# GLA and mLSTM values in a hybrid decoder layer: feature tiles transposed on TensorE in place of token tiles with meta passes

## The chip, the cores and the metric

One core of a Trainium2 chip runs the whole layer. The metric is the device time of one execution in microseconds (us); the time before is the median of three runs.

## What is computed

The input is 512 tokens of width 1024, with 16 learned meta tokens put ahead of them, so 528 rows go through the layer. One projection `z = rms_norm(h) @ w_in + b_in` feeds three mixers (GLA, sparse attention, mLSTM) and three gates. Cut to what matters:

```python
z = xn @ p["w_in"] + p["b_in"]          # 528 x 9696, split into the parts below
# GLA: 4 heads, dk = 128, dv = 256
o = q exp(G) S + (q decay k) v          # S collects k exp(..) v over the chunks
# mLSTM: 4 heads, dk = 128, dv = 256; q, k through a causal convolution and silu
h = (w_inter q C + P v) / max(|den|, exp(-m))   # P = decay * (q k^T)
mix = sig(gate_a) (gla @ w_br_gla) + sig(gate_b) (dsa @ w_br_dsa) + sig(gate_c) (ml @ w_br_ml)
h = h + rms_norm(mix @ w_out); h = h + rms_norm(relu(rms_norm(h) @ w_up)^2 @ w_down)
```

The values `v` of GLA and of mLSTM are 1024 columns of `w_in` each, 256 a head. Everything is float32, to float32 accuracy.

## The kernel before

**Precision.** Every large product is made of three matmuls in the faster float32 format: weight high part by activation high part, high by low, low by high (`whi`, `wlo`, `xh`, `xl`). Smaller products and all transposes are plain float32.

**Weights.** SP loads chunks of 512 KB into three raw buffers (`wraw`). GpSimd splits each one (L619 the high part, L623 the low part in four pieces) into one of four pairs of buffers, in the order of `plan()` (L135 to L286). It may start when the last tile that used the buffers has signalled `gemm_done` (L616 to L618). The DMA of a raw buffer waits for `split_done` (L535).

**Tiles.** A tile is a product into one of two PSUM slots `GP`, in turn (L144 to L149). It waits until its slot is empty (`gfree`, L1857) and its chunk split (L1859), and signals `gemm_done` (L1897). Kinds:
- F, features by tokens: the stationary operand is a weight block of 128 columns, the moving one the activations, 512 columns (L1873), or with `both` twice 264 columns, so that the meta tokens are among them (L1870). 8 blocks of the contraction by 3 parts.
- V, tokens by features: the stationary operand is 128 tokens, the moving one 256 weight columns (L1888). Tile A has the first two blocks of tokens, tile B the other two: 48 matmuls each.
- VM and VT (tile M): the 16 meta tokens of GLA, or the last 16 tokens for mLSTM, whose blocks begin at the first meta token. Their high and low parts lie side by side in `xm` (32 columns), so it takes 16 matmuls (L1879, L1880).
- G: the forget gate of GLA from rank 16 (L1894).

`all_values` (L224) makes A, B and M of a head from one pair of chunks. VectorE moves A and B to `vh` with the bias `vb` added (L1392) and M to `vm` (L1397).

**The order of the work** is written out by hand for each engine. `nxt(kind)` on TensorE runs the next head's tile of this kind, or in the last head a tile of the gates (`ta`, `tc`), so that projections fill the time in which other engines work for this head.
- GLA (L2204 to L2251), for each head: q and k of the next head, seven levels of decayed scores with projections between them, A of the next head around level 6, transposes of the decayed keys (L2235, L2237), B around the states (L2242 to L2247), M, then `weighted`, the output products (L2181).
- mLSTM (L2294 to L2326), for each head: q of the next head, scores 0 and 1, k of the next head, scores 2 and 3, A of the next head, the recalled products of scores and values (L2291, L2292), the sums over weights (L2322, L2324), then B and M of the next head.

ScalarE and VectorE have orders of their own. What the prediction's steps touch: on ScalarE the GLA loop (L929 to L961) with `off_out` (L879, keys out of PSUM), and the mLSTM loop (L1057 to L1087) with `conv_in` (L988), `conv_sig` (L996, sigmoid), `out_gate` (L1039), `lnexp` (L638, which loads the table for exp and ln) and `head_squares` (L1049). On VectorE `off` (L1489, its end are the states, L1502, L1508), the mLSTM loop (L1731 to L1756) with `weights_of` (L1688), `weight_sums` (L1696 to L1700), `conv` (L1658, L1660), `low_parts` (L1540) and `conv_mul` (L1671, L1673).

The part of the mLSTM loop of ScalarE that matters most:

```python
            if more:
                conv_sig(h + 1, 1)
            lnexp()
            if not more:
                gate_in("tc", 16, 2)
            head_squares(h)
```

Of the kernel before, what the change touches and what calls it, by code (L numbers as in the profile page):

```python
# [69 lines left out]
def _rows():  # L70
    at = 0
    for name, n, src in [
        ("gq", 4, "b_in"), ("gk", 4, "b_in"), ("gr", 8, "b_in"), ("cq", 2, "b_in"), ("ckv", 1, "b_in"),
        ("ik", 1, "b_in"), ("mq", 4, "b_in"), ("mk", 4, "b_in"), ("mo", 8, "b_in"), ("gate", 24, "b_in"),
        ("a2", 4, "b_gla_a"), ("hg", 2, "g_gla_head"),
        ("hm", 2, "g_ml_head"), ("dq", 2, "g_dsa_q"), ("dkv", 1, "g_dsa_kv"), ("ig", 1, "idx_ln_g"),
        ("ib", 1, "idx_ln_b"), ("fb", 1, "ml_f_bias"), ("cv", 32, "ml_conv"),
    ]:
        ROWS[name] = at
        ROW_LIST.append((name, n, src))  # L80
        at += n
    return at
# [6 lines left out]
JOINED = {"gq": 8, "cq": 3, "mq": 8}  # L89
FOLLOWS = ("gk", "ckv", "mk")  # L90
# [21 lines left out]
NROWDMA = 22  # L112
# [22 lines left out]
def plan():  # L135
# [27 lines left out]
    def values(name, c0):  # L163
        c = [chunk("w_in", c0, P), chunk("w_in", c0 + P, P)]
        assert c[0] % 2 == 0
        tile(name + "A", c, 0, kind="V", off=0)
        tile(name + "B", c, 0, kind="V", off=2)
        tile(name + "M", c, 2, kind="VT" if name[0] == "m" else "VM")

    def pad():  # L170
        if len(chunks) % 2:
            chunks.append(None)

# [50 lines left out]
    def all_values(name, c0):  # L224
        pad()
        values(name, c0)

    gla(0)
    all_values("gv0", C_GV)
    for h in range(HEADS):  # L230
        if h + 1 < HEADS:
            gla(h + 1)
        else:
            gates("ta", C_GATE, 0, 2)
        pairs("gr", C_GR, h)
        if h + 1 < HEADS:
            all_values(f"gv{h + 1}", C_GV + (h + 1) * DV)
# [6 lines left out]
    all_values("mv0", C_MV)  # L244
    for h in range(HEADS):
        if h + 1 < HEADS:
            feature(f"mq{h + 1}", "w_in", C_MQ + (h + 1) * DK, both=True)
            feature(f"mk{h + 1}", "w_in", C_MK + (h + 1) * DK, both=True)
        else:
            gates("tc", C_GATE + 2 * D, 0, 2)  # L250
        if h + 1 < HEADS:
            all_values(f"mv{h + 1}", C_MV + (h + 1) * DV)
# [37 lines left out]
def build(nc, a, line, scratch, rows, out):  # L290
# [3 lines left out]
    with ctx:  # L294
# [6 lines left out]
        def region(offset, specs):  # L301
# [23 lines left out]
        xm = sb("xm", [P, KT, 2 * META], F32R)  # L325
# [44 lines left out]
        (sgate, gtmp, vb, qh, ATm, kh, vh, vm, AT, sqo, rso, on, km) = region(AO, [  # L370
            ("sgate", [P, 2, SEQ], FP32), ("gtmp", [P, 2, SEQ], FP32), ("vb", [P, D], FP32),
# [3 lines left out]
        BO = AO + (2 * SEQ * 2 + D + 2 * SEQ + 2 * ALL + 2 * QT * DV + 2 * DV + QT * SEQ + SEQ + 2 * SEQ + SEQ + 2 * SEQ + 2 * P) * 4  # L375
# [16 lines left out]
        (sqr,) = region(AO + (7 * SEQ + D + 2 * ALL + 2 * QT * DV + 2 * DV + QT * SEQ) * 4, [("sqr", [P, 2, SEQ], F32R)])  # L392
        (qg,) = region(AO + (4 * SEQ + D) * 4, [("qg", [P, 2, QT, P + P // 2], FP32)])
# [17 lines left out]
        def gate_store(m):  # L411

            return [vh[:, 0, 0:2, :].rearrange("p a b -> p (a b)"), vh[:, 0, 2:4, :].rearrange("p a b -> p (a b)"),
                    kh[:, 0, 0:SEQ], qh[:, 0, :], vb[:, 0:SEQ], vb[:, SEQ:D], AT[:, 0, :], AT[:, 1, :]][m]
# [61 lines left out]
        ld_v, zpad, cv_ok, cs_ok, qk_ok = sem("ld_v"), sem("zpad"), sem("cv_ok"), sem("cs_ok"), sem("qk_ok")  # L476
# [3 lines left out]
        xt_ok, ml_c = sem("xt_ok"), sem("ml_consts")  # L480
# [147 lines left out]
        def _(act):  # L628
# [41 lines left out]
            def input_high(t):  # L670

                if t == QT:
# [3 lines left out]
                    act.wait_ge(xh_ok, KT + 1)  # L676
                    nc.scalar.activation(xm[:, :, 0:META], xh[:, :, 0:META].bitcast(FP32), ACT.Copy).then_inc(xh_ok, 1)
# [167 lines left out]
            act.dma_start(vb[:, :], a["b_in"][0:1, C_GV:C_GV + D].broadcast_to([P, D])).then_inc(ld_a, 16)  # L845
# [81 lines left out]

            gate_of(0)
            for h in range(HEADS):  # L929
                last = h == HEADS - 1  # L930
                level(h, 0)
                if h:
                    squared(h - 1)
                level(h, 1)
# [20 lines left out]
                off_out(h)  # L955
                sigmoids(h)
                if last:

                    whole("gv3M")
# [20 lines left out]
            act.dma_start(vb[:, :], a["b_in"][0:1, C_MV:C_MV + D].broadcast_to([P, D])).then_inc(ld_v, 16)  # L980
# [64 lines left out]
            fetch_maxima(0)  # L1045
            def head_squares(h):
# [10 lines left out]
            for h in range(HEADS):  # L1057
# [27 lines left out]
                if not more:  # L1085
                    gate_in("tc", 16, 2)
                head_squares(h)  # L1087
            gate_in("tc", 16, 3)
            whole("mv3M")
# [88 lines left out]
        def _(dve):  # L1178
# [45 lines left out]
            def input_low(t):  # L1224
                if t == QT:
# [3 lines left out]
                    dve.wait_ge(xl_ok, KT + 1)  # L1229
                    nc.vector.tensor_copy(xm[:, :, META:2 * META], xl[:, :, 0:META].bitcast(FP32)).then_inc(xl_ok, 1)  # L1230
# [155 lines left out]
            dve.wait_ge(ld_a, 48)  # L1386

            def values(name, h, part):
                if part < 2:
                    t = tl[f"{name}{h}{'AB'[part]}"]  # L1390
                    ps = ready(f"{name}{h}{'AB'[part]}")
                    tt(vh[:, h % 2, 2 * part:2 * part + 2, :], ps[:, 0:2 * DV].rearrange("p (t n) -> p t n", t=2),  # L1392
                       vb[:, h * DV:(h + 1) * DV].unsqueeze(1).broadcast_to([P, 2, DV]), ALU.add).then_inc(gfree[t.slot], 1)
                    return
                ps = ready(f"{name}{h}M")
                dve.wait_ge(f16_ok, 2)
                stt(vm[0:2 * META, h % 2, :], vb[0:2 * META, h * DV:(h + 1) * DV], first16[:, :], ps[0:2 * META, 0:DV], ALU.mult, ALU.add).then_inc(gfree[tl[f"{name}{h}M"].slot], 1)  # L1397
# [91 lines left out]
            def off(h):  # L1489
# [6 lines left out]
                if h + 1 < HEADS:  # L1496
                    values("gv", h + 1, 0)
# [55 lines left out]
            for part in range(3):  # L1553
                values("gv", 0, part)
            for h in range(HEADS):
# [33 lines left out]
                if more:  # L1589
                    values("gv", h + 1, 1)  # L1590
                    values("gv", h + 1, 2)
# [5 lines left out]
            def gate_rows_of(m):  # L1597
# [18 lines left out]
                if m == 3:  # L1616
                    dve.wait_ge(gemm_done, tl["gv3M"].val)
                    nc.vector.tensor_copy(xm[:, :, 0:META], xh[:, :, SEQ:ALL].bitcast(FP32)).then_inc(xt_ok, 1)
                    nc.vector.tensor_copy(xm[:, :, META:2 * META], xl[:, :, SEQ:ALL].bitcast(FP32)).then_inc(xt_ok, 1)
# [4 lines left out]
                if m == 5:  # L1624
                    nc.vector.tensor_copy(later[:, 0:DIAG[0]], later_bigT[:, META:P])
# [102 lines left out]
            dve.wait_ge(ld_v, 16)  # L1728
            for part in range(3):
                values("mv", 0, part)  # L1730
# [110 lines left out]
        def _(pe):  # L1841
# [9 lines left out]
            def gemm(name, part=None):  # L1851
# [22 lines left out]
                elif t.kind in ("V", "VM", "VT"):  # L1874
                    s0 = chunks[t.chunks[0]]["hl"]
                    if t.kind != "V":
                        for k in range(KT):
                            w = slice(k * P, (k + 1) * P)
# [574 lines left out]
```

## Time and profile before

| | us |
|---|---|
| median of 3 runs | 1264.04 (1263.27 to 1264.69) |
| the profiled execution | 1264.5 |
| its span, first to last instruction | 1261.8 |

Busy time in the span:

| engine | us | share |
|---|---|---|
| TensorE matmul | 1253.5 | 99% |
| TensorE weight load (beside matmuls) | 1029.2 | 82% |
| GpSimd | 772.8 | 61% |
| VectorE | 629.2 | 50% |
| ScalarE | 392.9 | 31% |

PE is TensorE's matmul, PEld its weight load, DVE VectorE, ACT ScalarE, POOL GpSimd; L1888 is line 1888 of the kernel before. Matmuls overlap: a printed duration runs from the start of one to its modelled end, and the next one starts earlier, so the time that a matmul takes of the engine is the distance between starts. Plain float32 matmuls are two records each, transposes one.

### The profile page before, as it was taken

How to read it: one execution, taken by the hardware profiler on the slowest of the kernel's cores; microseconds unless marked ns; L12 is line 12 of the kernel's file. 1: busy time of each engine (PE TensorE's matmuls, PEld its weight loads, DVE VectorE, ACT ScalarE, POOL GpSimd, SP SyncE). 2: the span in 40 equal slices, each digit the busy share in tenths (PEclk: the TensorE clock that was granted, in tenths of full speed). 3: DMA queues.
4: the chain of work that ended last, by engine and by line, in shares of the span. 5: the costliest groups of instructions: out<-in, count | busy, mean ns of one | idle time of the engine just before them, and what ended most of it. 6: DMA issues, size and time to landing. Idle time of an engine off the chain costs nothing.

```text
span 1261.8 us, 17439 instructions
## 1 busy us (share of the span) xinstructions
PE 1253.5 (99%) x6561; PEld 1029.2 (82%) x6564; DVE 629.2 (50%) x1115; ACT 392.9 (31%) x810; POOL 772.8 (61%) x914
## 2 busy tenths in 40 slices
PE   9999999999999999999999999999999999999998
PEld 8866887677899899888899987887888888888886
DVE  4368888642276886835447773342511112333434
ACT  5343565533023323333024343312511111221322
POOL 8746430125584753758775556784876677888882
PEclk9999999999999999999999999999999999999999
DMA  7847200223231322322433333522233333232321
GB/s 177 241 122 224 68 1 26 68 67 94 71 97 51 84 62 56 84 68 84 117 110 78 86 97 100 188 95 84 84 101 100 85 100 105 96 100 84 101 84 67
DMA packets 167433, 120.08 MB, mean 95 GB/s; under 512 B 11367, under 2 KB 145613, under 8 KB 167350
## 3 DMA queue, kind: packets, MB, share of 16 engines
q1 hardware_dynamic: 160612, 107.79, 29.7%
q10 hardware_dynamic: 6738, 11.18, 2.7%
q8 instruction: 52, 0.85, 0.3%
q14 instruction: 31, 0.25, 0.1%
HBM read 114.71 MB, written 9.62 MB: 99 GB/s over the span
## 4 chain that ended last, share of the span: by engine, by line
PE 99%; DVE 0%; ACT 0%; issue 0%; DVEq 0%; ACTq 0%
PE GP L1873 46%; PE GP L1909 9%; PE PA L1909 9%; PE GP L1888 7%; PE GP L1870 6%; PE PA L2073 3%; PE GP L2135 3%; PE PA L2173 1%; PE PA L2110 1%; PE PA L2291 1%; PE GP L2366 1%; PE GP L1954 1%; PE PA L2043 1%; PE PA L2283 1%; PE PA L2074 1%; PE GP L1880 1%
## 5 line engine op out<-in xcount | busy, mean ns | idle before, releaser
L623 POOL TENSOR_TENSOR wlo<-wraw,whi 128x256 fp32r<-128x256 f32 x708 | 564.7, 828 | 14.7
L619 POOL TENSOR_SCALAR whi<-wraw 128x1024 fp32r<-128x1024 f32 x177 | 201.1, 1136 | 449.9 <-PE GP L1873 227.2
L1873 PE MATMUL GP<-xh,whi 128*128 128x512 f32 x352 | 144.8, 411 | 0.0
L1873 PE MATMUL GP<-xh,wlo 128*128 128x512 f32 x352 | 139.1, 395 | 0.0
L1873 PE MATMUL GP<-xl,whi 128*128 128x512 f32 x352 | 138.8, 394 | 0.0
L1815 DVE TENSOR_TENSOR ul<-U,uh 128x512 fp32r<-128x512 f32 x64 | 65.2, 1054 | 109.5 <-ACT uh L1157 109.5
L1873 PE MATMUL GP<-nh,whi 128*128 128x512 f32 x240 | 95.1, 396 | 0.0
L1873 PE MATMUL GP<-nl,whi 128*128 128x512 f32 x240 | 95.1, 396 | 0.0
L1873 PE MATMUL GP<-nh,wlo 128*128 128x512 f32 x240 | 95.1, 396 | 0.0
L1819 DVE SCALAR_TENSOR_TENSOR U<-GP,rrow 128x512 f32<-128x512 f32 x32 | 22.1, 692 | 141.7 <-PE GP L1873 140.3
L1873 PEld LDWEIGHTS GP<-xh,whi 128*128 128x128 f32 x352 | 66.2, 188 | 16.0 <-issue 1.5
L1873 PEld LDWEIGHTS GP<-xh,wlo 128*128 128x128 f32 x352 | 66.1, 188 | 15.2
L1873 PEld LDWEIGHTS GP<-xl,whi 128*128 128x128 f32 x352 | 66.3, 188 | 14.3 <-issue 0.5
L1157 ACT ACTIVATE uh<-U 128x512 fp32r<-128x512 f32 x64 | 37.2, 625 | 129.0 <-PE PA L1909 70.4
L1873 PE MATMUL GP<-yh,whi 128*128 128x512 f32 x192 | 76.3, 397 | 0.0
L1873 PE MATMUL GP<-yl,whi 128*128 128x512 f32 x192 | 76.1, 396 | 0.0
L1873 PE MATMUL GP<-yh,wlo 128*128 128x512 f32 x192 | 76.1, 396 | 0.0
L1888 PE MATMUL GP<-whi,xh 128*128 128x256 f32 x256 | 74.6, 292 | 0.2 <-DVE kh L1403 0.2
L1888 PE MATMUL GP<-wlo,xh 128*128 128x256 f32 x256 | 71.9, 281 | 0.0
L1888 PE MATMUL GP<-whi,xl 128*128 128x256 f32 x256 | 71.7, 280 | 0.0
L1161 ACT ACTIVATE U<-U 128x512 f32<-128x512 f32 x32 | 20.2, 632 | 152.9 <-DVE U L1819 152.9
L1873 PEld LDWEIGHTS GP<-nh,wlo 128*128 128x128 f32 x240 | 45.2, 188 | 11.0
(426 smaller groups left out, 2771.5 us busy)
## 6 DMA issues: line engine op xcount, KB each, us to landing
wraw<-in_w_in SPq DMA_DIRECT2D x75, 512.0 KB, 3.9
wraw<-in_w_up SPq DMA_DIRECT2D x32, 512.0 KB, 4.0
wraw<-in_w_down SPq DMA_DIRECT2D x32, 512.0 KB, 3.5
line_rows<-bias_line SPq DMA_DIRECT2D x8, 655.0 KB, 5.1
table<-line_rows SPq DMA_DIRECT2D x4, 1024.0 KB, 5.6
wraw<-in_w_br_dsa SPq DMA_DIRECT2D x8, 512.0 KB, 4.2
wraw<-in_w_br_gla SPq DMA_DIRECT2D x8, 512.0 KB, 3.9
wraw<-in_w_br_ml SPq DMA_DIRECT2D x8, 512.0 KB, 4.0
```

The costliest lines, as they stand in the source:

```text
L619: nc.gpsimd.tensor_scalar(hi, src, 1.0, 1.0, ALU.mult, ALU.mult).then_inc(hi_done, 1)
L623: part = nc.gpsimd.tensor_tensor(lo[:, at:to], src[:, at:to], hi[:, at:to].bitcast(FP32), ALU.subtract)
L1157: nc.scalar.activation(uh[:, k % 4, :], U[:, k % FT, :], ACT.Copy).then_inc(uh_ok, 1)
L1161: nc.scalar.activation(U[:, m, :], U[:, m, :], ACT.Square).then_inc(U_ok, 1)
L1815: tt(ul[:, k % 4, :], U[:, k % FT, :], uh[:, k % 4, :].bitcast(FP32), ALU.subtract).then_inc(ul_ok, 1)
L1819: stt(U[:, m, :], ps[:, 0:SEQ], 0.0, rrow[:, :], ALU.max, ALU.mult).then_inc(gfree[tl[f"up{m}"].slot], 1)
L1870: ins = mm(ps[0:t.m, b * SEQ:b * SEQ + HALF], wt[:, s0, w], hx[:, k, b * HALF:(b + 1) * HALF], start=st, stop=sp_)
L1873: ins = mm(ps[0:t.m, 0:SEQ], wt[:, s0, w], av, start=st, stop=sp_)
L1888: ins = mm(o_, at_[:, k, tok], wt[:, s0:s0 + 2, k * P:(k + 1) * P], start=(k == 0 and p_ == 0), stop=(k == KT - 1 and p_ == 2))
L1909: ins = mm(accumulators(name, hf, i), av[:, i * P:(i + 1) * P], wt[:, c["hl"], k * SEQ:(k + 1) * SEQ], start=(n == 0 and k == 0 and p_ == ...
L2073: mm(bank(v % 2)[0:r, 0:w], qlat[:, h, TILE_AT[i]:TILE_AT[i + 1]], kvT[:, 0:w], start=True, stop=False)
L2135: ins = mm(pairs_of(o_, g), kvn[:, j, :], pairs_of(PT[:, g % 2, j, :], g), start=(j == 0), stop=(j == i))
```

## The change

The values become F tiles with `both`, two of 128 features for a head (`gv00`, `gv01`, ...), with the meta tokens among their 528 columns. ScalarE copies each to a new buffer `vT` and adds the bias there (`value_in`). A new kind of tile T transposes `vT` on TensorE in four blocks of 128 tokens and one of 16 columns (the meta tokens for GLA, the last tokens for mLSTM), five transposes into a slot of `GP`; it waits for the copy of its F tile (`evacuated`). The T tiles are copied to `vh` and `vm` by VectorE, in GLA the second half by ScalarE (`values_copied`). Tiles V, VM and VT, `xm`, `vb`, its two broadcast DMAs and the pairing of chunks go; the biases of values and of two more row groups come with rows that are loaded anyway, so SP issues 20 row DMAs in place of 22. Cut to its core:

```diff
+    def turned(name, v):
+        tile(f"{name}T{v}", [], 0, kind="T")
...
+    def value(name, c0, h, v):
+        feature(f"{name}{h}{v}", "w_in", c0 + (2 * h + v) * P, both=True)
...
     def input_high(t):
...
-                    act.wait_ge(xh_ok, KT + 1)
-                    nc.scalar.activation(xm[:, :, 0:META], xh[:, :, 0:META].bitcast(FP32), ACT.Copy).then_inc(xh_ok, 1)
...
-            act.dma_start(vb[:, :], a["b_in"][0:1, C_GV:C_GV + D].broadcast_to([P, D])).then_inc(ld_a, 16)
...
+            def value_in(name, h, v):
+
+                if h:
+                    act.wait_ge(gemm_done, tl[f"{name}{h - 1}T{v}"].val)
+                t = tl[f"{name}{h}{v}"]
+                nc.scalar.activation(two(vT[:, v, :]), halves(ready(f"{name}{h}{v}")), ACT.Identity,
+                                     bias=cc(name, 2 * h + v)).then_inc(gfree[t.slot], 1)
+
+            def values_copied(h):
+
+                ps = ready(f"gv{h}T1")
+                nc.scalar.activation(vh[:, h % 2, :, P:DV], ps[:, 0:SEQ].rearrange("p (t n) -> p t n", t=QT), ACT.Copy)
+                nc.scalar.activation(vm[0:META, h % 2, P:DV], ps[0:META, SEQ:SEQ + P], ACT.Copy).then_inc(gfree[tl[f"gv{h}T1"].slot], 1)
...
             gate_of(0)
+            value_in("gv", 0, 0)
+            value_in("gv", 0, 1)
             for h in range(HEADS):
                 last = h == HEADS - 1
                 level(h, 0)
                 if h:
                     squared(h - 1)
+                values_copied(h)
                 level(h, 1)
...
                 off_out(h)
+                if not last:
+                    value_in("gv", h + 1, 0)
                 sigmoids(h)
+                if not last:
+                    value_in("gv", h + 1, 1)
...
+            value_in("mv", 0, 0)
+            value_in("mv", 0, 1)
...
                 if more:
                     conv_sig(h + 1, 1)
                 lnexp()
-                if not more:
+                if more:
+                    value_in("mv", h + 1, 0)
+                else:
                     gate_in("tc", 16, 2)
                 head_squares(h)
+                if more:
+                    value_in("mv", h + 1, 1)
...
+            def values(name, h, v):
+
+                ps, c = ready(f"{name}{h}T{v}"), slice(v * P, (v + 1) * P)
+                nc.vector.tensor_copy(vh[:, h % 2, :, c], ps[:, 0:SEQ].rearrange("p (t n) -> p t n", t=QT))
+                nc.vector.tensor_copy(vm[0:META, h % 2, c], ps[0:META, SEQ:SEQ + P]).then_inc(gfree[tl[f"{name}{h}T{v}"].slot], 1)
...
                 masked(h)
                 if h:
                     head_scaled(h - 1)
+                values("mv", h, 1)
                 for j in range(2):
                     weights_of(h, j)
...
                     conv(h + 1, 1)
-                    values("mv", h + 1, 0)
                     conv_mul(h + 1, 1)
                 denominator(h)
                 head_sums(h)
                 if more:
-                    for part in range(1, 3):
-                        values("mv", h + 1, part)
+                    values("mv", h + 1, 0)
...
+                elif t.kind == "T":
+                    v, first = int(name[4]), 0 if name[0] == "m" else META
+                    few = slice(SEQ, ALL) if name[0] == "m" else slice(0, META)
+                    evacuated(name[0:3] + name[4])
+                    for i in range(QT):
+                        nc.tensor.transpose(ps[:, i * P:(i + 1) * P], vT[:, v, first + i * P:first + (i + 1) * P], ident[:, :])
+                    ins = nc.tensor.transpose(ps[0:META, SEQ:SEQ + P], vT[:, v, few], ident[:, :])
...
-                nxt("gvA", 0)
+                nxt("gv0", 0)
                 level(h, 6)
-                nxt("gvA", 1)
+                nxt("gv0", 1)
...
-                nxt("gvB", 0)
+                nxt("gv1", 0)
...
-                nxt("gvB", 1)
-                nxt("gvM")
+                nxt("gv1", 1)
+                nxt("gvT0")
                 pe.wait_ge(od_q, 6 * h + 6)
                 weighted(h).then_inc(av_ps, 1)
+                if h + 1 < HEADS:
+                    gemm(f"gv{h + 1}T1")
...
                 nxt("mq", 1)
+                gemm(f"mv{h}T1")
...
-                nxt("mvA")
+                nxt("mv0")
                 pe.wait_ge(at_ok, 5 * h + 5)
...
-                nxt("mvB")
-                nxt("mvM")
+                nxt("mvT0")
+                nxt("mv1")
```

## Rows read from the trace of the kernel before

**Rows 1.** The page: busy time of the engines, and TensorE's granted clock in 40 slices.
```profile
PE 1253.5 (99%) x6561; PEld 1029.2 (82%) x6564; DVE 629.2 (50%) x1115; ACT 392.9 (31%) x810; POOL 772.8 (61%) x914
...
PEclk9999999999999999999999999999999999999999
```

**Rows 2.** Waits of TensorE, longest first: us in total, times, longest us.
```profile
PE PA L1930 <- DVE ones L1202: 1.2, 1, 1.2
```

**Rows 3.** Timeline of TensorE, mLSTM's third loop: start us, us, engine, line, operation, operands, count.
```profile
718.11 0.41 PE L1870 MATMUL GP<-xl,whi 128*128 128x264 f32 x2
...
720.78 1.69 PE L2283 MATMUL PA<-qh,kh 128*128 128x512 f32 x4
...
729.19 0.28 PE L1888 MATMUL GP<-wlo,xh 128*128 128x256 f32 x1
...
734.72 2.39 PE L2291 MATMUL PA<-AT,vh 128*128 128x512 f32 x8
...
740.22 0.59 PE L1888 MATMUL GP<-whi,xh 128*128 128x256 f32 x1
...
746.19 0.28 PE L1879 MATMUL GP<-whi,xm 128*32 128x256 f32 x1
...
748.04 0.40 PE L1873 MATMUL GP<-xh,whi 128*128 128x512 f32 x1
```

**Rows 4.** Timeline of TensorE in GLA: transposes of the keys, and the matmul behind.
```profile
445.25 0.30 PE L2235 MATMUL PA<-ident,km 128*128 128x128 f32 x1
...
445.39 0.49 PE L2237 MATMUL PA<-ident,KHt 128*128 128x128 f32 x3
...
445.64 0.36 PE L1888 MATMUL GP<-whi,xh 128*128 128x256 f32 x1
```

**Rows 5.** Timelines of TensorE and ScalarE, mLSTM's first and second loop.
```profile
673.12 0.59 PE L1888 MATMUL GP<-whi,xh 128*128 128x256 f32 x1
...
674.95 1.03 ACT L1049 ACTIVATE sqo<-PA 128x1024 f32<-128x1024 f32 x1
...
706.67 0.59 PE L1888 MATMUL GP<-whi,xh 128*128 128x256 f32 x1
...
708.91 1.03 ACT L1049 ACTIVATE sqo<-PA 128x1024 f32<-128x1024 f32 x1
```

**Rows 6.** Timelines of VectorE and ScalarE, mLSTM's third loop.
```profile
735.53 1.29 DVE L1540 TENSOR_TENSOR yl<-on,yh 128x512 fp32r<-128x512 f32 x2
...
738.09 2.38 DVE L1660 SCALAR_TENSOR_TENSOR cv<-zc,col,cv 128x528 f32<-128x528 f32 x3
...
736.20 0.68 ACT L988 ACTIVATE zc<-GP,col 128x528 f32<-128x528 f32 x1
...
740.50 0.65 ACT L996 ACTIVATE sgc<-cv 128x528 f32<-128x528 f32 x1 [2.58 <-DVE cv L1660]
...
741.17 1.28 ACT L638 ACT_TABLE_LOAD   x1
...
742.46 1.03 ACT L1049 ACTIVATE sqo<-PA 128x1024 f32<-128x1024 f32 x1
```

**Rows 7.** Timelines of VectorE and GpSimd, beside a split, and GpSimd's wait.
```profile
543.37 2.69 DVE L1540 TENSOR_TENSOR yl<-on,yh 128x512 fp32r<-128x512 f32 x2
...
630.56 3.45 DVE L1660 SCALAR_TENSOR_TENSOR cv<-zc,col,cv 128x528 f32<-128x528 f32 x3
...
630.32 4.29 POOL L623 TENSOR_TENSOR wlo<-wraw,whi 128x256 fp32r<-128x256 f32 x4
...
748.37 1.87 POOL L619 TENSOR_SCALAR whi<-wraw 128x1024 fp32r<-128x1024 f32 x1 [14.92 <-PE GP L1880]
```

**Rows 8.** Timelines of ScalarE, VectorE and TensorE, GLA's second loop.
```profile
445.92 0.60 ACT L879 ACTIVATE AT<-PA 128x512 f32<-128x512 f32 x1 [5.86 <-PE PA L2237]
...
450.08 1.58 DVE L1508 SCALAR_TENSOR_TENSOR AT<-AT,gf,PA 128x256 f32<-128x256 f32 x3
...
453.13 0.28 PE L1879 MATMUL GP<-whi,xm 128*32 128x256 f32 x1
```

More of the change, by code:

```diff
@@ L222, in gates @@
             feature(f"{name}{m}", "w_in", c0 + m * P)
-    def all_values(name, c0):
-        pad()
-        values(name, c0)
+    def value(name, c0, h, v):
+        feature(f"{name}{h}{v}", "w_in", c0 + (2 * h + v) * P, both=True)
     gla(0)
-    all_values("gv0", C_GV)
+    value("gv", C_GV, 0, 0)
+    value("gv", C_GV, 0, 1)
+    turned("gv0", 0)
+    turned("gv0", 1)
     for h in range(HEADS):
@@ L243, in plan @@
     feature("mk0", "w_in", C_MK, both=True)
-    all_values("mv0", C_MV)
+    value("mv", C_MV, 0, 0)
+    value("mv", C_MV, 0, 1)
+    turned("mv0", 0)
     for h in range(HEADS):
-        if h + 1 < HEADS:
+        more = h + 1 < HEADS
+        if more:
             feature(f"mq{h + 1}", "w_in", C_MQ + (h + 1) * DK, both=True)
+        else:
+            gates("tc", C_GATE + 2 * D, 0, 1)
+        turned(f"mv{h}", 1)
+        if more:
             feature(f"mk{h + 1}", "w_in", C_MK + (h + 1) * DK, both=True)
-        else:
-            gates("tc", C_GATE + 2 * D, 0, 2)
-        if h + 1 < HEADS:
-            all_values(f"mv{h + 1}", C_MV + (h + 1) * DV)
+            value("mv", C_MV, h + 1, 0)
+            turned(f"mv{h + 1}", 0)
+            value("mv", C_MV, h + 1, 1)
+        else:
+            gates("tc", C_GATE + 2 * D, 1, 2)
     gates("tc", C_GATE + 2 * D, 2, 8)
@@ L1084, in _ @@
                 lnexp()
-                if not more:
+                if more:
+                    value_in("mv", h + 1, 0)
+                else:
                     gate_in("tc", 16, 2)
                 head_squares(h)
+                if more:
+                    value_in("mv", h + 1, 1)
             gate_in("tc", 16, 3)
-            whole("mv3M")
             gate_in("tc", 16, 4)
@@ L1552, in _ @@
             forget_sums(0)
-            for part in range(3):
-                values("gv", 0, part)
+            values("gv", 0, 0)
             for h in range(HEADS):
@@ L1727, in _ @@
             dve.wait_ge(ml_c, 2)
-            dve.wait_ge(ld_v, 16)
-            for part in range(3):
-                values("mv", 0, part)
+            values("mv", 0, 0)
             for h in range(HEADS):
@@ L2268, in _ @@
             gemm("mk0")
-            for nm in ("mv0A", "mv0B"):
+            for nm in ("mv00", "mv01", "mv0T0"):
                 gemm(nm)
-            pe.wait_ge(xt_ok, 2)
-            gemm("mv0M")
             pe.wait_ge(M_ok, 1)
@@ L2298, in nxt @@
                     else:
-                        gemm({"mq": "tc0", "mk": "tc1", "mvA": "tc2", "mvB": "tc3", "mvM": "tc4"}[kind], part)
+                        gemm({"mq": "tc0", "mk": "tc1", "mv0": "tc2", "mvT0": "tc3", "mv1": "tc4"}[kind], part)
                 pe.wait_ge(qk_ok, 2 * h + 2)
```

95 lines of the change are left out of this document (26 added, 69 removed).

## Prediction

> **What bounds the kernel now.** The page comes first. TensorE is busy 1253.5 of the 1261.8 us span, the next engine 772.8 us, and the granted clock is at its full level (2.4 GHz) in all 40 slices [rows 1]. The list of waits, asked for TensorE alone, then shows that its longest wait is 1.2 us, at the start [rows 2]. So no wait sets this time, only TensorE's own stream: what leaves the stream comes off, and every new wait in it is paid in full, since nothing behind it has slack to give back. I therefore count pitches (start to start) in TensorE's timeline, not the printed durations, which overlap. Then I ask of each new wait in the stream when its releaser is ready.
>
> **1. Meta passes out.** A head's pass is 16 matmuls, from 746.19 to the next tile at 748.04 [rows 3]: 1.85 us. Eight heads: -14.8 us.
>
> **2. Values in feature layout.** A head has 96 matmuls either way: two 128-wide tiles of 8 x 3 x 2 halves, against four token tiles of 8 x 3. They stream 264 columns instead of 256. Pitch before: 47 matmuls between 729.19 and 734.72, 0.118 us. A tile that is already in the new form: 22 matmuls between 718.11 and 720.78, 0.121 us [rows 3]. Over 768 matmuls at 3.7 ns: +2.8 us.
>
> **3. Transposes in.** There are two tiles of five per head, 16 tiles. The nearest rows are the four transposes of the decayed keys, 445.25 to 445.64, so 0.39 us, the last three in 0.25 [rows 4]. A fifth adds 0.08; the matmul behind them shows 0.36 instead of 0.28, a change-over. I take 0.50 us a tile, +8.0 us. Below: five at 0.083, 0.41 us (+6.6). Above: 0.39 + 0.08 + 0.08 + as much again ahead of them, and a bit for two waits, 0.70 us (+11.2).
> The printed duration of one of these transposes is 0.30 us [rows 4], and at 0.27 to 0.30 each, if they did not overlap, 80 of them would be some 22 us. The Trainium skill (TensorE: Matmul & The Clock Gate, Part 4) speaks against this change there: about 275 ns for a transpose in a kernel's context. By it the sum would be 14 us higher. The trace has three inside 0.25 us, so I go by the pitch and keep the rule as a rival.
>
> Parts 1 to 3: -4.0 us of stream.
>
> **4. The new wait, mLSTM.** For heads 1 to 3 the tile mvT0 stands right behind the recalled products and the sums over weights, where the second half of the token tiles stood: at 673.12, 706.67 and 740.22 [rows 5, 3]. It may start only when ScalarE has copied the feature tile into vT. In ScalarE's queue that copy stands behind the sigmoid of the second convolution and the table load. That sigmoid starts at 740.50 and the load at 741.17; the next instruction, before which the new copy is put, starts at 742.46 [rows 6]. The copy has the shape of the conv input copy, 128x528 out of PSUM, 0.68 us [rows 6]; with its hand-over I take 0.70. vT is ready at 743.16. TensorE is there at 740.22 + 0.16 (48 columns x 8 longer, part 2) = 740.38. It waits 2.8 us. In the other heads the instruction behind the load starts at 674.95 and 708.91 [rows 5]: 675.65 - 673.28 = 2.4 and 709.61 - 706.83 = 2.8. Together +7.9 us. None of it is covered: the next tile (mv1) stands behind the transposes in TensorE's queue, and needs the slot that the same copy frees. The fourth head has gates there and doesn't wait. The chain to that sigmoid (scores, weights, their sums, two convolutions on VectorE) is not edited, so it does not come sooner.
>
> **5. What stretches that chain.** GpSimd splits the next weights when a chunk's last tile is done. Before, the pair of a head's values was held until the meta pass had run; GpSimd then waited 14.92 us for it [rows 7]. Now the first value tile's chunk comes free when that tile ends, at about 734.72 + 0.16 [rows 3], in the midst of VectorE's chain. Beside a split VectorE is slower: three convolution steps took 3.45 us while GpSimd split (630.3 to 634.6) and 2.38 us without [rows 7, 6]; the two subtractions to yl took 2.69 us beside a split and 1.29 us in this chain [rows 7, 6]. Both in full: +1.4 and +1.1 us in the second and third loop, +1.1 in the first, which has no subtractions; with the small steps up to 6.5 us in all. Below it is 0. A split is 4.3 us of subtractions behind a rounding of up to 1.87 [rows 7], so it ends about where the chain did; the last steps of a chain that has been stretched run alone. I take two thirds, +4.5 us.
>
> **6. GLA and the starts.** There the copy of the first half is put behind the key copy, 445.92 to 446.52 [rows 8], so vT is ready at 447.3, ahead of T0 at about 453.3, where the meta pass stood (453.13 and 0.17 for the longer columns) [rows 8]. The second half's copy ends 0.7 us behind its tile, and T1 stands behind the 32 output products, which are longer than that. VectorE's states end at 451.66 [rows 8] and are needed behind T0, at 453.8; that 2.1 us has to take in a split that now begins with the end of the first value tile, ahead of 445.25 [rows 4]. ScalarE's extra copies, two of 0.68 [rows 6], one of 0.60 [rows 8] and a small one a head, stand where it waits for VectorE; VectorE loses a pass over 128x512 a head. I cost all this at nothing; if the 2.1 us did not do, it would be up to 1 us a head. The two starts have no such work between: T1 of head 0 waits for a copy that can start only when its tile ends (0.7 against a T0 of 0.5), the next tile waits for VectorE to empty T0, and in mLSTM mq1 waits for the slot of mv01 in the same way. Each 0.2 to 0.3: +0.8 us, between 0 and 1.5. Queues: SP issues two row DMAs fewer, ScalarE's two broadcasts of the value biases go, and with them VectorE's copies to xm; no TensorE wait stood on any of them, so nothing.
>
> **Sum:** -4.0 + 7.9 + 4.5 + 0.8 = +9.2 us. The profiled execution took 1264.5 us (span 1261.8), 0.5 above the median of 1264.04; on the median this is **1273.2 us**, slower.
>
> **Rivals.**
> - *No stretch*: the wait is as worked out, but the split costs the chain nothing. +4.7, 1268.7 us. For it: the rows with a split have it beside the whole step, here it may run out early.
> - *The wait isn't there*, the side of faster: ScalarE's copy is done when TensorE arrives. Its place is the one of part 4; it decides at a chain 2.8 us shorter. Then -4.0 + 0.8 = -3.2, 1260.8 us. For it: VectorE drops an addition of 128x512 from this part of its queue. Against it: that addition stands behind the sigmoid's releaser, so its loss shortens nothing ahead.
> - *The clock falls* in the three waits of 4 us or so. TensorE has no wait over 1.2 us now and the clock stays at full level [rows 1, 2], so no row gives the price. Bounds: 0, and the value tile behind each wait (5.8 us) at half speed, 17.4 us. Half of it: 1282 us. The Trainium skill has such a rule (same page, "Why this matters for your kernels"): long idle gaps of TensorE between bursts of matmuls bring back the half clock, so they are to be avoided. By it this case would be likelier the more part 5 adds to the waits; no row here shows it.
> - *Transposes at their printed duration*: +13.8, 1287 us. Against it: three in 0.25 us [rows 4].
> - That the change doesn't do what it says: the stream without the meta passes is in the diff, 128 matmuls of 6561 [rows 1]; I see no way that they stay.
>
> **How the numbers follow.** A measurement of this kernel tells apart about 0.2%, 2.5 us. Forecast 0.55, no stretch 0.2, clock 0.08, no wait 0.07, transposes 0.03; the last 0.07 for sums that happen to land near zero, waits half hidden. Even the low ends (transposes at 0.41, no stretch) leave -5.4 + 7.9 + 0.8 = +3.3, above 2.5, so the first two cases count as slower. Slower 0.86, same 0.06, faster 0.08. Range: the low end is no stretch with the cheapest transposes, 1267.3; the high end takes full stretch and transposes at 0.70 (+5.2) and the mild part of the clock's case: 1267 to 1280.
>
> **What would show it.** Right: TensorE's list of waits has three entries at the transposes' line, released by ScalarE's value copy, of 2.4 us and up, and none above 0.5 in GLA; the meta pass's lines are gone; five transposes take 0.5 us; the convolution steps beside a split take over 1 us each. Wrong: no wait at that line, or the clock below full level behind it, or a wait in GLA at the output products.

## The result, and the profile after

| | before | after |
|---|---|---|
| median of the runs, us | 1263.76 (1263.27 to 1264.69, 4 runs) | 1280.83 (1279.81 to 1283.10, 4 runs) |
| span of the profiled execution, us | 1261.8 | 1279.0 |
| mean granted clock of TensorE | 1.000 | 0.993 |

The changed kernel takes 1.0135 times as long (95% interval 1.0122 to 1.0148): 17.1 us slower, where 9.2 were forecast and 1280 was the top of the range. The direction and the place were right, the size was not.

The page after the change, the answer to [rows 1]: TensorE's busy time, the slices of the granted clock, and the chain that ended last.

```profile
PE 1256.7 (98%) x6513; PEld 1031.2 (81%) x6516; DVE 617.5 (48%) x1112; ACT 405.4 (32%) x833; POOL 774.2 (61%) x914
...
PEclk9999999999999999999999889999999999999999
...
PE 95%; DVE 3%; ACT 1%; issue 1%; DVEq 0%; ACTq 0%
```

Two things are new. Two slices show the clock below full, both in mLSTM (a slice is 32 us; the two run from 703 to 767 us, and the one before them, with 0.95, still prints as a 9). And the chain that ended last runs through VectorE for 3% of the span, where TensorE alone had set the end.

The first of TensorE's list of waits, ahead of the one of [rows 2] (waiting line, releaser, us in total, times, longest):

```profile
PE GP L1885 <- ACT vT L933: 13.5, 4, 4.9
```

The wait that part 4 named is there: the transposes' line, released by ScalarE's copy into vT. TensorE's timeline at the three places, the answer to [rows 3, 5] (rounds one, two and three below are the first three passes of the mLSTM loop; start, us, engine, line, operation, operands, count, and in brackets the idle time with its releaser). L2322 is the last of the sums over weights, L1885 the transposes of T0, L2192 the squares in the middle of the next query's projection; the last row is the first gate tile behind mv31.

```profile
672.08 0.85 PE L2322 MATMUL PA<-Wd,ones 128*128 128x400 f32 x2
676.25 0.63 PE L1885 MATMUL GP<-ident,vT 128*128 128x128 f32 x4 [3.32 <-ACT vT L933]
...
687.12 0.40 PE L2192 MATMUL PA<-sqr,onesr 128*128 128x512 f32 x1
...
710.30 0.85 PE L2322 MATMUL PA<-Wd,ones 128*128 128x400 f32 x2
716.07 1.09 PE L1885 MATMUL GP<-ident,vT 128*128 128x128 f32 x4 [4.92 <-ACT vT L933]
...
727.75 0.40 PE L2192 MATMUL PA<-sqr,onesr 128*128 128x512 f32 x1
...
750.96 0.85 PE L2322 MATMUL PA<-Wd,ones 128*128 128x400 f32 x2
756.73 1.08 PE L1885 MATMUL GP<-ident,vT 128*128 128x128 f32 x4 [4.92 <-ACT vT L933]
...
765.63 0.40 PE L1879 MATMUL GP<-xh,whi 128*128 128x512 f32 x1
```

Before, the row that follows the sums started 0.38 us behind them (739.84 to 740.22). Now it is 4.17, 5.77 and 5.77 us. The difference is what TensorE loses: 3.8 + 5.4 + 5.4 = **14.6 us**. (The brackets say 0.47 less each, since they count from the modelled end of the matmul before.) The four transposes took 1.08 us in the third round, and in GLA, behind no wait, 0.60; so something else is slower too. Two windows of 11 us, around and behind the transposes of the second and the third round: width, busy times of PE, PEld, DVE, ACT and POOL, granted clock, DMA share, GB/s.

```profile
715.00:726.00 11.00, 9.93 (x63) 9.88 (x64) 5.13 (x10) 3.25 (x7) 0.84 (x1) 0.72 0.00 1
...
755.00:766.00 11.00, 9.27 (x55) 9.17 (x56) 5.76 (x12) 3.12 (x5) 0.04 (x1) 0.69 0.00 1
```

TensorE's clock was at its lower level (1.2 GHz) for a good part of each stretch: 0.72 and 0.69 on average. What it cost is read further down against a kernel that does the same work at the full level: 6.4 us.

VectorE, GpSimd and ScalarE in the third round, the answer to [rows 6]:

```profile
746.46 2.67 DVE L1554 TENSOR_TENSOR yl<-on,yh 128x512 fp32r<-128x512 f32 x2
749.05 1.21 DVE L1680 SCALAR_TENSOR_TENSOR qh<-cv,sgc 128x512 f32<-128x512 f32 x1
750.40 0.74 DVE L1667 TENSOR_SCALAR cv<-zc,col 128x528 f32<-128x528 f32 x1
751.17 2.73 DVE L1669 SCALAR_TENSOR_TENSOR cv<-zc,col,cv 128x528 f32<-128x528 f32 x3
...
746.17 1.28 POOL L622 TENSOR_SCALAR whi<-wraw 128x1024 fp32r<-128x1024 f32 x1 [1.80 <-PE GP L1876]
747.53 4.19 POOL L626 TENSOR_TENSOR wlo<-wraw,whi 128x256 fp32r<-128x256 f32 x4
...
753.93 0.64 ACT L1014 ACTIVATE sgc<-cv 128x528 f32<-128x528 f32 x1 [5.09 <-DVE cv L1669]
754.59 1.28 ACT L641 ACT_TABLE_LOAD   x1
755.89 0.70 ACT L933 ACTIVATE vT<-GP,col 128x528 f32<-128x528 f32 x1
```

GpSimd begins its split at 746.17, released by the first values' tile, and ends it at 751.72, and VectorE's steps beside it are long: the two subtractions to yl 2.67 us against 1.29 [rows 6], the three convolution steps 2.73 against 2.38. ScalarE's copy stands behind the sigmoid and the table load as worked out, and ends 0.14 us ahead of T0.

### The profile page after: what moved, and what is told of

Same layout as the page of the kernel before. It is cut to its first block, busy times and chain, and to the rows that moved or that the text cites. A ratio compares the mean times of both kernels' runs of the same rounds, so it can differ in the third digit from the quotient of the medians.

```text
span 1279.0 us, 17360 instructions
## 1 busy us (share of the span) xinstructions
PE 1256.7 (98%) x6513; PEld 1031.2 (81%) x6516; DVE 617.5 (48%) x1112; ACT 405.4 (32%) x833; POOL 774.2 (61%) x914
## 4 chain that ended last, share of the span: by engine, by line
PE 95%; DVE 3%; ACT 1%; issue 1%; DVEq 0%; ACTq 0%
PE GP L1879 45%; PE GP L1876 13%; PE GP L1906 9%; PE PA L1906 9%; PE PA L2070 3%; PE GP L2132 3%; PE PA L2170 1%; PE PA L2107 1%; DVE cv L1669 1%; PE GP L2364 1%; PE GP L1951 1%; PE PA L2040 1%; PE PA L2280 1%; PE PA L2071 1%; PE GP L1885 1%
## 5 line engine op out<-in xcount | busy, mean ns | idle before, releaser
L626 POOL TENSOR_TENSOR wlo<-wraw,whi 128x256 fp32r<-128x256 f32 x708 | 578.1, 847 | 14.8
L622 POOL TENSOR_SCALAR whi<-wraw 128x1024 fp32r<-128x1024 f32 x177 | 188.6, 1066 | 465.7 <-PE GP L1879 247.8
L1876 PE MATMUL GP<-xh,whi 128*128 128x264 f32 x480 | 104.5, 299 | 0.7 <-ACT vT L933 0.4
L1876 PE MATMUL GP<-xl,whi 128*128 128x264 f32 x480 | 99.6, 290 | 0.0
L1876 PE MATMUL GP<-xh,wlo 128*128 128x264 f32 x480 | 99.1, 288 | 0.0
L1876 PEld LDWEIGHTS GP<-xh,whi 128*128 128x128 f32 x480 | 77.6, 195 | 4.4 <-issue 2.1
L1879 PEld LDWEIGHTS GP<-xh,whi 128*128 128x128 f32 x352 | 66.2, 188 | 16.6 <-issue 1.8
L1879 PEld LDWEIGHTS GP<-xh,wlo 128*128 128x128 f32 x352 | 66.1, 188 | 15.5
L1879 PEld LDWEIGHTS GP<-xl,whi 128*128 128x128 f32 x352 | 66.4, 189 | 14.2 <-issue 0.5
L1876 PEld LDWEIGHTS GP<-xl,whi 128*128 128x128 f32 x480 | 76.7, 194 | 0.0
L1876 PEld LDWEIGHTS GP<-xh,wlo 128*128 128x128 f32 x480 | 76.4, 193 | 0.0
```

Of the source, the lines that this page charges most:

```text
L622: nc.gpsimd.tensor_scalar(hi, src, 1.0, 1.0, ALU.mult, ALU.mult).then_inc(hi_done, 1)
L626: part = nc.gpsimd.tensor_tensor(lo[:, at:to], src[:, at:to], hi[:, at:to].bitcast(FP32), ALU.subtract)
L1876: ins = mm(ps[0:t.m, b * SEQ:b * SEQ + HALF], wt[:, s0, w], hx[:, k, b * HALF:(b + 1) * HALF], start=st, stop=sp_)
L1879: ins = mm(ps[0:t.m, 0:SEQ], wt[:, s0, w], av, start=st, stop=sp_)
```

## The experiments

Differences in time are against the changed kernel's 1280.83 us unless said otherwise; ratios are against the kernel before. The kernel before was run beside each group, at 1264.34, 1264.06 and 1263.98 us.

### ScalarE's copy early

```diff
                 if more:
+                    value_in("mv", h + 1, 0)
                     conv_sig(h + 1, 1)
                 lnexp()
-                if more:
-                    value_in("mv", h + 1, 0)
-                else:
+                if not more:
                     gate_in("tc", 16, 2)
```

> Edit: in the mLSTM loop ScalarE copies vT (first half) before the second convolution sigmoid of the round instead of behind it and the table load. Own theory: the loss of 17 us against the kernel before is three waits of TensorE ahead of the mLSTM transposes (3.8 + 5.4 + 5.4 = 14.6 us, the copy being queued behind the sigmoid) and the half clock that follows each (about 6.5 us). With the copy early both go: 1280.8 - 14.6 - 6.5 = about 1260 us, granted clock 1.00 throughout, the three waits under 0.5 us. Rival 1, the clock falls because of the transposes and not of the gap before them: the waits go, the half clock stays, about 1266. Rival 2, something else in the chain (the sigmoid being 0.7 us later, the next scores) takes the wait's place: 1270 or more, with a new wait at another line.

Measured: **1273.51 us**, ratio 1.0075 (1.0062 to 1.0087). Rival 2 was right. No wait is left ahead of the transposes, but TensorE's list has these instead:

```profile
PE GP L1875 <- DVE vm L1411: 4.8, 2, 3.7
PE GP L1878 <- DVE vm L1411: 3.7, 1, 3.7
```

The tile after next (mq, in the last round a gate) needs the slot of T0, and VectorE empties T0 only at the end of its chain. The second round, TensorE and VectorE:

```profile
718.13 0.48 PE L1875 MATMUL GP<-xh,whi 128*128 128x264 f32 x2 [3.66 <-DVE vm L1411]
...
714.65 1.30 DVE L1723 CAST sqr<-sqo 128x512 fp32r<-128x512 f32 x1
715.99 1.09 DVE L1724 TENSOR_TENSOR sqr<-sqo,sqr 128x512 fp32r<-128x512 f32 x1
...
717.60 0.27 DVE L1411 COPY vm<-GP 16x128 f32<-16x128 f32 x1
```

The waits are 1.1, 3.7 and 3.7 us, and the clock falls behind the long ones as it did before (0.84 over 715 to 726 us). So ScalarE's place in the queue was only the nearest reason. VectorE's chain stands behind it, and whoever ends it late is waited for.

### The split held back

```diff
+    for h in range(1, HEADS):
+        chunks[tiles[f"mv{h}0"].chunks[0]]["end"] = tiles[f"mv{h}1"].val
```

> Edit: the weight buffer of the first values' chunk of heads 1 to 3 is released with the second values' tile, so that GpSimd does not split in it while VectorE runs the second convolution. Own theory: the split stretches VectorE's steps from 2.4 to 3.4 us and 0.5 to 0.7 us; without it the three waits fall from 3.8, 5.4 and 5.4 us to about 2.4, 2.8 and 2.8, which is 6.6 us less: 1274 us if the clock falls as now, down to 1268 if gaps of this size leave it whole. Rival, the stretch has another cause than GpSimd or the held split collides elsewhere: 1280 to 1281, convolution steps still above 3 us.

Measured: **1271.80 us**, ratio 1.0059 (1.0046 to 1.0072). The same rows of VectorE, and the waits of the three rounds:

```profile
740.96 1.29 DVE L1557 TENSOR_TENSOR yl<-on,yh 128x512 fp32r<-128x512 f32 x2
742.16 0.68 DVE L1683 SCALAR_TENSOR_TENSOR qh<-cv,sgc 128x512 f32<-128x512 f32 x1
742.98 0.49 DVE L1670 TENSOR_SCALAR cv<-zc,col 128x528 f32<-128x528 f32 x1
743.51 2.38 DVE L1672 SCALAR_TENSOR_TENSOR cv<-zc,col,cv 128x528 f32<-128x528 f32 x3
...
675.57 0.63 PE L1888 MATMUL GP<-ident,vT 128*128 128x128 f32 x4 [2.02 <-ACT vT L936]
...
711.39 0.63 PE L1888 MATMUL GP<-ident,vT 128*128 128x128 f32 x4 [2.41 <-ACT vT L936]
...
748.72 0.63 PE L1888 MATMUL GP<-ident,vT 128*128 128x128 f32 x4 [2.42 <-ACT vT L936]
```

With the 0.47 that the brackets leave out, the waits are 2.5, 2.9 and 2.9 us: 8.3 in all. So the split's share of the 14.6 is 6.3 us. It can be seen step by step in the third round: 1.38 + 0.53 + 0.25 + 0.35 = 2.5 us in the four rows of VectorE, and 5.4 - 2.9 = 2.5 in the wait. The clock stayed at its full level behind the first gap and fell behind the other two.

### The order of two tiles swapped

```diff
-                nxt("mvT0")
                 nxt("mv1")
+                nxt("mvT0")
```

(and the same in the plan of tiles)

> Edit: in the mLSTM loop TensorE runs the second values' tile (5.9 us at full clock) before the transposes of the first, so the copy of ScalarE and all that is ahead of it lie beside matmuls. Nothing else moves. Own theory: waits and half clock go as with the early copy, with up to 0.3 us in each round for the slot that the next query's projection now shares with the second values' tile: 1260 to 1261 us. The longest wait (5.4 us) is only 0.5 us shorter than its new cover. Rival 1, the clock falls through the transposes: about 1266. Rival 2, the wait only moves to the next projection's slot: 1270 or more, a wait at L1876.

Measured: **1266.92 us**, ratio 1.0019 (1.0010 to 1.0028). The cover is long enough: no wait for the copy of the first half, the clock full in the three rounds. But 6 us more stay than expected. The second round:

```profile
715.03 0.48 PE L1876 MATMUL GP<-xh,whi 128*128 128x264 f32 x2 [0.67 <-ACT vT L933]
...
723.02 1.80 PE L2280 MATMUL PA<-qh,kh 128*128 128x512 f32 x4 [0.89 <-ACT rso L646]
```

The slot costs 0.7 to 0.8 us a round instead of 0.3, since ScalarE can copy the second half only when its tile has ended and only 0.55 us of transposes lie between. And rso, at the end of what VectorE's sums release, is late by some 1 us in two rounds. These waits make 4.6 us by the starts of the rows, and the program's start took 0.9 us more (last section).

### The waits filled

```diff
                 elif t.kind == "T":
...
+                    for _ in range({"mv1T0": 15, "mv2T0": 22, "mv3T0": 22}.get(name, 0)):
+                        mm(ps[:, 5 * P:6 * P], ones[:, :], ones[:, :], start=True, stop=True)
```

> Edit: 15, 22 and 22 matmuls of ones by ones (128 x 128, some 0.22 us each) stand in the three waits ahead of the mLSTM transposes and write columns that nothing reads; the waits for ScalarE's copy stay. Own theory: the copy comes at the same time, so TensorE is late by the same 14.6 us, but the clock stays full: 6.5 us less than now, about 1274.5 us, granted clock 1.00. Rival 1, the half clock is not due to the gap: 1280 to 1281 with the clock still down behind the waits. Rival 2, the filling is longer than the waits and costs itself: above 1276 with a full clock.

Measured: **1274.87 us**, ratio 1.0086 (1.0072 to 1.0100), as the own theory had it. The third round:

```profile
748.25 5.08 PE L1884 MATMUL GP<-ones 128*128 128x128 f32 x44
753.22 0.66 PE L1887 MATMUL GP<-ident,vT 128*128 128x128 f32 x4
```

T0 starts no sooner (the idle time is full of matmuls that nothing reads), the clock is 1.00 throughout, and 6.0 us are gone. What the half clock costs is thus separated from the wait itself: the one is 6 us, the rest of the loss is the waits.

### The GLA transposes three times

```diff
-                    for i in range(QT):
+                    for i in list(range(QT)) * (3 if name[0] == "g" else 1):
```

> Edit, on the changed kernel: each of the eight GLA transposed tiles does its four 128 x 128 transposes three times, 64 transposes more in all; nothing waits in these tiles by the trace. It measures the term of the forecast that prices the transposes. By the pitch in the trace (four in 0.435 us, 0.109 us each): 64 x 0.109 = 7.0 us more, 1287.8 us. Rival, each costs its printed duration of about 0.28 us, or stalls for its weight load: some 18 us more, 1298 to 1299. Second rival, the longer tiles make VectorE's copies late and GLA waits for them: above 1290, with new waits in GLA. In sentences apart: the Trainium skill, TensorE: Matmul & The Clock Gate, Part 4, gives about 275 ns for such a transpose, which would give 17.6 us.

Measured: **1289.30 us**, +8.5 us. Twelve transposes and the fifth behind them:

```profile
406.07 1.47 PE L1885 MATMUL GP<-ident,vT 128*128 128x128 f32 x12
407.38 0.27 PE L1886 MATMUL GP<-ident,vT 128*16 128x128 f32 x1
```

From 406.07 to 407.38 is 1.31 us for twelve, 0.109 us each: 7.0 us for the 64. The rest is the start of the program (first 26 matmuls in 5.55 us instead of 4.68) and a half clock in mLSTM that lasted about 1 us longer. The printed duration of one (0.28 us) overlaps that of its neighbours, and is not what it costs in a row. The Trainium skill (TensorE: Matmul & The Clock Gate, Part 4) gives about 275 ns for a 128x128 transpose in one kernel's context. The duration printed here agrees with it. As the cost of transposes that stand one behind the other it is two and a half times too high, and there the measurement decides.

### Early copy and held split together

The two diffs above, both.

> Edits: the early copy of the first run and the held split of the second, together. The first run (early copy alone) moved the wait: TensorE's waits of 1.1, 3.7 and 3.7 us now stand after the second values' tile, for VectorE's copies of the transposed half, which stand at the end of its chain, with about 3.3 us of half clock. Own theory: the chain of VectorE is what bounds the round, and without the split it ends 1.3, 2.5 and 2.5 us sooner (the differences between the waits with and without the hold): waits of about 0, 1.2 and 1.2 us, full clock: 1273.5 - 6.1 - 3.3 = 1264.1 us. Rival, the two edits overlap because the early copy already runs beside the split: no gain over the hold alone, 1271 to 1272.

Measured: **1261.57 us**, ratio 0.9983 (0.9974 to 0.9991): faster than the kernel before. Neither edit alone comes under 1271, and the two together gain 19.3 us, more than the sum of 7.3 and 9.0. What the theory had wrong is the remainder: it expected waits of 1.2 us in two rounds, and there are none (none of TensorE is above 0.4 us once the program has started up). The second round of VectorE shows why:

```profile
710.85 0.43 DVE L1726 CAST sqr<-sqo 128x512 fp32r<-128x512 f32 x1
711.31 0.69 DVE L1727 TENSOR_TENSOR sqr<-sqo,sqr 128x512 fp32r<-128x512 f32 x1
```

With the early copy alone, the cast and the subtraction took 1.30 and 1.09 us, beside another split, which the end of mv's second tile sets off. Now the chain ends before that one begins. It was shortened twice, by 2.5 and by 1.3 us, and the second could not be read from the two kernels that the expectation compared.

### Early copy and VectorE's copies before the denominators

```diff
+                if more:
+                    values("mv", h + 1, 0)
                 denominator(h)
                 head_sums(h)
-                if more:
-                    values("mv", h + 1, 0)
```

> Edits: ScalarE's copy early, and VectorE's two copies of the transposed half moved from behind the head's sums of squares to before its denominators; the split is not held. Own theory: the slot is free in time, so the waits for the copies (8.5 us) and the half clock (3.3 us) go; the sums of squares come 0.95 us later in a chain that GpSimd still stretches, and TensorE meets them in the middle of the query's projection, with up to 1 us of wait in two rounds, at the squares' line or for rso: 1273.5 - 11.8 + 0 to 2 = 1262 to 1264. Rival: the whole 3.7 us waits reappear at the squares or behind them, 1270 or more, since the chain is as long as before and only its order differs.

Measured: **1265.65 us**, ratio 1.0014 (1.0006 to 1.0023). The waits are where they were expected, a little longer:

```profile
PE PA L2191 <- DVE sqr L1724: 1.9, 2, 1.0
PE PA L2279 <- ACT rso L646: 1.4, 2, 0.7
```

The chain is as long as with the early copy alone, but its part for which TensorE waited 3.7 us is now done first, and the part behind it is late by 1.0. Order alone won 7.9 us.

### All three

The diff above on top of the early copy and the held split.

> Edits: the early copy, VectorE's copies before the denominators, and the held split. Own theory: the chain is 1.3 to 2.5 us shorter than in the run without the hold, so neither the copies nor the squares are late: no wait of TensorE above 0.3 us in the mLSTM rounds, clock 1.00, and the change's own gain comes through: 1280.8 - 14.6 (waits) - 6.5 (half clock) = 1259.7, or about 1260 to 1261, 3 to 4 us under the kernel before (1264.3). Rival: the next scores or the root of the head's norm (rso) become the end and 2 to 4 us stay, 1263 or more, no faster than before.

Measured: **1261.55 us**, ratio 0.9980 (0.9971 to 0.9989), no better than without the last edit. The same three stretches of TensorE as in the profile after, from T0 to the squares (third: to the gate):

```profile
673.36 0.60 PE L1887 MATMUL GP<-ident,vT 128*128 128x128 f32 x4
...
682.69 0.40 PE L2194 MATMUL PA<-sqr,onesr 128*128 128x512 f32 x1
...
706.57 0.60 PE L1887 MATMUL GP<-ident,vT 128*128 128x128 f32 x4
...
715.89 0.40 PE L2194 MATMUL PA<-sqr,onesr 128*128 128x512 f32 x1
...
739.79 0.60 PE L1887 MATMUL GP<-ident,vT 128*128 128x128 f32 x4
...
746.19 0.40 PE L1881 MATMUL GP<-xh,whi 128*128 128x512 f32 x1
```

9.33, 9.32 and 6.40 us at full clock, against 10.87, 11.68 and 8.90 in the changed kernel: 1.5 + 2.4 + 2.5 = **6.4 us** is the price of the half clock there. The run also measures parts 1 to 3 with the starts: 1261.55 - 1264.06 = -2.5 us, where -3.2 was worked out.

One more thing is in its timeline. In the third round the last sums (L2324) start at 739.10 and T0 at 739.79, 0.69 us behind them with nothing to wait for, where the value tile of the kernel before followed after 0.38. It is the same in the other two rounds. So 0.3 us of each of the three distances in the profile after isn't waiting: against this run the waits are 13.7 us and not 14.6, and the 0.9 us between the two are already in the -2.5.

### Shorter gaps

The filling again, with fewer matmuls, so that gaps of chosen length stay behind it:

```diff
-                    for _ in range({"mv1T0": 15, "mv2T0": 22, "mv3T0": 22}.get(name, 0)):
+                    for _ in range({"mv1T0": 6, "mv2T0": 13, "mv3T0": 13}.get(name, 0)):
```

and 4, 11 and 11 in the second kernel.

> Edit, on the changed kernel: 6, 13 and 13 matmuls of ones by ones (0.227 us each at full clock, as measured with the longer filling) at the start of the three waits of 3.8, 5.4 and 5.4 us, so that TensorE stands idle for only about 2.4 us in each. The run with the held split had gaps of 2.5 us (clock stayed full) and twice 2.9 us (it fell). Theory A, the length of the gap decides: the clock stays full behind all three, 6.5 us less than the changed kernel, 1274.3 us. Theory B, the gap of the second and third round costs the clock whatever its length, through what runs around it: only 1.6 us less, about 1279.

> As the run before, with 4, 11 and 11 matmuls, which leave gaps of about 2.9 us. Theory A, the length decides: the clock falls behind all three as it fell behind the two gaps of 2.9 us with the held split, by 1.5 us each: 1274.3 + 4.5 = about 1279. Theory B, the place decides: full behind the first, half behind the others, about 1277.5. Between these the granted clock behind the first gap is what tells.

Measured: **1277.37** and **1277.23 us**, ratios 1.0103 (1.0086 to 1.0120) and 1.0103 (1.0088 to 1.0118). The gaps came out shorter than planned, by the brackets 1.9 us in the one kernel and 2.4 in the other. The first two rounds of the one, and the first of the other (its second and third have 2.37 and 2.36):

```profile
676.23 0.65 PE L1887 MATMUL GP<-ident,vT 128*128 128x128 f32 x4 [1.91 <-ACT vT L933]
...
715.99 0.66 PE L1887 MATMUL GP<-ident,vT 128*128 128x128 f32 x4 [1.92 <-ACT vT L933]
```

```profile
676.48 0.66 PE L1887 MATMUL GP<-ident,vT 128*128 128x128 f32 x4 [2.37 <-ACT vT L933]
```

The windows of the first kernel behind these two gaps:

```profile
676.00:687.00 11.00, 10.77 (x76) 10.75 (x77) 4.72 (x10) 4.00 (x9) 2.38 (x3) 0.84 0.09 27
...
715.00:726.00 11.00, 10.01 (x81) 9.91 (x82) 5.14 (x10) 4.75 (x10) 3.16 (x5) 1.00 0.11 25
```

And of the second kernel behind its first gap:

```profile
676.00:687.00 11.00, 10.53 (x75) 10.51 (x76) 4.97 (x10) 4.15 (x9) 2.14 (x3) 0.84 0.10 31
```

Behind the third gap (755 to 766 us) the granted clock is 0.84 in the first kernel and 1.00 in the second. Both theories fall. A gap of 1.91 us cost the clock and one of 1.92 did not. It fell in rounds one and three of the first kernel and in round one alone of the second; with the held split it stayed in round one and fell in the others. So neither the length alone nor the place alone decides between 1.9 and 2.4 us.

Each of these patterns is read from one profile, and another execution of the same kernel may show another. The four executions of the changed kernel went from 1279.81 us at a mean granted clock of 0.994 to 1283.10 us at 0.992, while the eleven with the early copy and the held split lie within 1.2 us. And the profiled execution of the second kernel above took 1276.25 us, the other three 1277.11 to 1277.64: they may have lost the clock once more. No second profile was taken that could show it.

## Why the prediction was wrong, step by step

Two terms of the sum failed. The half clock behind the waits stood in it at nothing and cost 6.4 us; the stretch by GpSimd stood in it at 4.5 us and cost 6.3. The waits themselves, the direction and the place were right.

| term, us | forecast | measured | by |
|---|---|---|---|
| stream and starts | -3.2 | -2.5 | all three edits against the kernel before |
| wait for ScalarE's copy | +7.9 | +8.3 | the held split |
| stretch by GpSimd | +4.5 | +6.3 | 14.6 less 8.3 |
| half clock | 0 | +6.4 | the same stretches at full clock |
| sum | +9.2 | +18.5 | the runs say +17.1 |

The terms come out 1.4 us above the runs. The 0.3 us that T0 starts later in each round even without a wait are counted twice, in the first line and in the second: 0.9 us. And the first 26 matmuls took 5.31 us in the profile of the run with all three edits, 4.68 in the profile after: 0.6 us.

- **Bound, parts 1 to 3 and the starts (-3.2):** right; -2.5 measured once the waits are gone. The transposes' term held: where no wait is near, four take 0.44 us and the fifth 0.11, so 0.55 for a tile against 0.50 taken, with 0.3 more behind the sums in three rounds, which was not seen; the rival that priced them at their printed duration is refuted by the tripled ones.
- **Part 4, the new wait (+7.9):** right in place, releaser and size. With the split out of the way it measured 8.3 us (2.5, 2.9, 2.9, for 2.4, 2.8, 2.8).
- **Part 5, the stretch (+4.5):** right in mechanism, mis-sized. It measured 6.3, just under its upper end of 6.5. The step that failed is "I take two thirds". Its reason, that the chain's last steps run alone, held in two rounds: the split that began at 746.17 ended at 751.72, early in the three convolution steps, and they lost 0.35 us where 1.1 were the full price. But the two subtractions lost their full 1.4, and the two small steps between, put at some 0.4 us for all rounds together, lost 0.78 in each of these rounds (0.53 + 0.25). And in the first round the convolution steps lay beside the split for most of their time and lost 1.0 (3.41 us, against 2.38 with the split held):

```profile
670.01 3.41 DVE L1669 SCALAR_TENSOR_TENSOR cv<-zc,col,cv 128x528 f32<-128x528 f32 x3
```

The Trainium skill (SBUF — State Buffer, "Who interferes with whom") says that a VectorE instruction with two SBUF inputs contends with a GpSimd instruction that reads SBUF. The trace agrees: the steps with two such inputs went from 0.64 to 1.34 us each (yl) and from 0.68 to 1.21 (qh). A step with one, L1667, slowed as well, from 0.49 to 0.74.

- **The clock (0):** the step that failed most. The sum had it at nothing, and the case that the clock falls was a rival of 0.08, as an alternative to the forecast. But in the changed kernel it fell behind each of the three waits, which the forecast itself put at some 4 us. It belonged in the sum, at its half price of 8.7; measured were 6.4 us by the rows and 6.0 by the filled waits. This is the term that left the range: without it the measured terms make -2.5 + 8.3 + 6.3 = +12.1, 1276 us, which lies inside.
- **Part 6, GLA (0):** right. TensorE's list shows nothing for GLA above 0.4 us, at its start.
- **"None of it is covered ... the next tile stands behind the transposes":** true, but it stopped one step short. It named what waits for T0, and not what empties T0. With the copy early, VectorE's copies at the end of its chain cost 8.5 us by themselves. The rival *the wait isn't there* had its number right (1260.8; 1261.6 measured) but not its condition: a copy that is done when TensorE arrives was not enough, the chain of VectorE had to be short as well.

Not settled: why the clock falls behind some gaps of 1.9 to 2.4 us and not behind others, and how often it does in other executions of the same kernel. Not tried: GLA's new form with mLSTM's old one.

## What to carry to other kernels

When a forecast puts a wait of some us into a TensorE that never waited, put the half clock behind it into the same sum: here some 14 us of waiting cost another 6.4. When a buffer is released sooner, look up what the engine that refills it will do next and beside whom; the split that began one tile earlier cost 6.3 us, and holding it back took one line. And of a new tile between engines ask both questions, who fills it and who empties it: the first fix only moved the wait from the one to the other, and it took both edits to turn a kernel that was 1.4% slower into one that is 0.2% faster.

## What the runs showed of the hardware

- Gaps of TensorE of 3.3 us and more (by the brackets: 3.3, 4.9, 4.9 in the changed kernel, the same in the run with tripled transposes, twice 3.7 with the early copy) brought the half clock eight times out of eight; gaps of 1.1 us and less never in these rounds; gaps of 1.9 to 2.4 us five times out of nine, at about 1.5 us each (by one profile of each kernel). The direction of the Trainium skill's rule on idle gaps (TensorE: Matmul & The Clock Gate, "Why this matters for your kernels") is borne out, but a gap need not be long to cost.
- Matmuls of ones by ones in the gap keep the clock at its full level, so a wait that can't be avoided can at least be made cheaper by 1.5 to 2.5 us.
- The start of the program isn't the same in every execution. The first 26 matmuls took 4.68 us in the changed kernel's profile, 5.09 before, 5.61 with the swapped order, 5.66 with the early copy and VectorE's copies moved. That is up to 1.0 us between two profiles that no edit explains. They come faster as they go (in the changed kernel 7 in the fourth microsecond, 10 in the sixth), although the view gives the granted clock as 1.00 there; at which level they ran isn't shown.
